# Decoder block on one core: front and attention in one program, first projections in another order, rotary turns later in the tails

## The reference, cut to what matters

```python
q = (rms_norm(cq, q_norm_w[l]) @ w_uq[l]).reshape(b, s, N_HEADS, QK_NOPE_DIM + QK_ROPE_DIM)
q_nope, q_rope = q[..., :QK_NOPE_DIM], q[..., QK_NOPE_DIM:]
kv = (rms_norm(ckv, kv_norm_w[l]) @ w_ukv[l]).reshape(b, s, N_HEADS, QK_NOPE_DIM + V_DIM)
k_nope, v = kv[..., :QK_NOPE_DIM], kv[..., QK_NOPE_DIM:]
q_rope = apply_rope(q_rope, cos[:, :, None, :], sin[:, :, None, :])
k_rope = apply_rope(k_pe, cos, sin)
o = mla_attention(q_nope, q_rope, k_nope, k_rope, v)   # causal softmax((qn.kn + qr.kr) * scale) @ v
y_b = (o * jax.nn.silu(b_gate)) @ w_attn_out[l]
```

## Time and profile before

| | us |
|---|---|
| median of 3 runs | 2596.09 (2595.48 to 2596.93) |
| the profiled execution's own time | 2595.87 |
| its span, first to last instruction | 2594.0 |
| PE busy | 2535.4 (98%) |
| DVE busy | 1709.9 (66%) |
| ACT busy | 875.0 (34%) |
| POOL busy | 689.2 (27%) |

### The profile page before, as it was taken

The page is one execution under the profiler, slowest core; times in us unless marked ns, Lnnn a source line. Parts: engine busy times, 40 slices in busy tenths (PEclk is TensorE's granted clock), DMA queues, the critical chain, the costliest instruction groups (busy, mean ns, idle before and its releaser), DMA issues. The chain is left out here.

```text
span 2594.0 us, 30760 instructions
## 1 busy us (share of the span) xinstructions
PE 2535.4 (98%) x12058; PEld 2092.6 (81%) x12058; DVE 1709.9 (66%) x2025; ACT 875.0 (34%) x1735; POOL 689.2 (27%) x621
## 2 busy tenths in 40 slices
PE   5999999999999999999999999999999999999998
PEld 4788888888888888788878888888888788888887
DVE  5678787989889898657466676676677522223343
ACT  3552111111111111133455655655656521111221
POOL 2223111111111111133133333333344310323422
PEclk9999999999999999999999999999999999999999
DMA  8023321313213121179824214214213264757532
GB/s 310 25 94 122 91 57 58 91 49 90 57 58 90 49 83 57 62 242 305 297 100 143 82 68 139 82 68 138 82 69 103 84 229 138 224 203 234 188 138 81
DMA packets 193180, 316.48 MB, mean 122 GB/s; under 512 B 14249, under 2 KB 107501, under 8 KB 182412
## 3 DMA queue, kind: packets, MB, share of 16 engines
q1 hardware_dynamic: 183164, 289.08, 34.2%
q0 software_dynamic: 5120, 16.78, 2.0%
q10 hardware_dynamic: 4752, 8.65, 0.9%
HBM read 207.52 MB, written 106.95 MB: 121 GB/s over the span
## 5 line engine op out<-in xcount | busy, mean ns | idle before, releaser
L52 PE MATMUL ps_proj<-h_hi,w_hi 128*128 128x512 f32 x1664 | 655.5, 394 | 9.2 <-DVE h_lo L937 6.8
L54 PE MATMUL ps_proj<-h_hi,w_lo 128*128 128x512 f32 x1664 | 648.8, 390 | 0.0
L53 PE MATMUL ps_proj<-h_lo,w_hi 128*128 128x512 f32 x1664 | 648.7, 390 | 0.0
L1046 DVE SCALAR_TENSOR_TENSOR acc<-u,taps_t,acc 128x2048 f32<-128x2048 f32 x240 | 628.9, 2621 | 8.5
L829 POOL TENSOR_TENSOR w_lo<-raw,w_hi 128x1024 fp32r<-128x1024 f32 x52 | 175.0, 3365 | 808.2 <-ACT w_hi L558 808.2
L52 PEld LDWEIGHTS ps_proj<-h_hi,w_hi 128*128 128x128 f32 x1664 | 312.9, 188 | 77.1 <-issue 7.5
L54 PEld LDWEIGHTS ps_proj<-h_hi,w_lo 128*128 128x128 f32 x1664 | 313.0, 188 | 65.6
L53 PEld LDWEIGHTS ps_proj<-h_lo,w_hi 128*128 128x128 f32 x1664 | 313.2, 188 | 65.3 <-issue 1.9
L2033 POOL TENSOR_SCALAR prob<-prob,rinv 128x512 f32<-128x512 f32 (+2 forms) x320 | 199.8, 642 | 348.3 <-DVE rinv L1916 345.3
L1977 DVE TENSOR_TENSOR pt_lo<-ps_t,pt_hi 128x512 fp32r<-128x512 f32 (+1 forms) x320 | 192.7, 607 | 76.6 <-ACT pt_hi L1894 72.8
L1960 DVE TENSOR_REDUCE nmax<-ps_ring 128x1 f32<-128x512 f32 (+3 forms) x288 | 176.2, 622 | 95.0 <-PE ps_ring L1760 77.0
(11 more groups left out here) (272 smaller groups left out, 4044.4 us busy)
## 6 DMA issues: line engine op xcount, KB each, us to landing
qlat<-qlat_dram SPq DMA_DIRECT2D x32, 1024.0 KB, 7.6
raw<-in_w_in_dram SPq DMA_DIRECT2D x52, 512.0 KB, 6.4
under_h<-in_w_ada_dram SPq DMA_DIRECT2D x8, 1024.0 KB, 10.7
ga_dram<-lat SPq DMA_DIRECT2D x8, 1024.0 KB, 5.0
gb_dram<-lat SPq DMA_DIRECT2D x8, 1024.0 KB, 5.2
agate_dram<-lat SPq DMA_DIRECT2D x8, 1024.0 KB, 5.0
conv_dram<-acc SPq DMA_DIRECT2D x8, 1024.0 KB, 3.9
v_dram<-v_st SPq DMA_DIRECT2D x4, 2048.0 KB, 8.9
```

The lines of the kernel that those rows point to most:

```text
L52: pe.matmul(out, wh, xh, start=first, stop=False)
L53: pe.matmul(out, wh, xl, start=False, stop=False)
L54: return pe.matmul(out, wl, xh, start=False, stop=last)
L1046: dve.scalar_tensor_tensor(acc[:], u[:, n:n + S], tap(n), acc[:], ALU.mult, ALU.add).then_inc(conv_tap if n < TAPS - 1 else conv_done, 1)
```

## The change

Front and attention no longer have blocks of their own. Each phase function now only defines its five engine programs, and one block runs on every engine first the front's and then the attention's, with no barrier between. In its place TensorE waits, at the first use of each of its eight banks in attention, for the front's unit that held it (`k.front_bank_free`), and ahead of the first scores for the loads of the rotated key (`k.rotary_key_in`). SyncE still waits at the end of the front's program for the front's transfers, as before; the semaphores of attention are taken from the shared set. The output phase keeps its block.

The first projections come in another order (`FIRST`): those of chunk 3's queries stand before the last two key chunks. The rotary turns stand behind units named in `TURNED`: chunk 2's behind `("QN", 3)`, chunk 3's behind `("K", 2)`, so that behind `("K", 3)` there is none; the one-column Exp with its table load follows the turn of chunk 3. On SyncE `queries(3)` is issued ahead of `store_values(1)`.

In the tail of a second body the turn of chunk 2 and `VS 0` leave the tiles: four T follow `QN 2`, then `QN 3`, `VS 0`, and the whole turns of chunk 2 and chunk 3. TensorE's order stays the same.

The rest of the diff is indentation; without it and without the signatures that change alike it is:

```diff
+Programs = namedtuple("Programs", "sync tensor scalar vector gpsimd")
...
-    FIRST = [(kind, c) for c in range(NC_) for kind in ("QR", "QN", "K")]
+    FIRST = [("QR", 0), ("QN", 0), ("K", 0), ("QR", 1), ("QN", 1), ("K", 1), ("QR", 2), ("QN", 2), ("QR", 3), ("QN", 3),
+             ("K", 2), ("K", 3)]
+    TURNED = {("K", 0): 0, ("K", 1): 1, ("QN", 3): 2, ("K", 2): 3}
...
             store_second(1)
-            store_values(1)
             queries(3)
+            store_values(1)
             rotary_key(1, k.kr_lo2)
...
-                if kind == "K":
-                    if n == 0:
+                if (kind, n) in TURNED:
+                    if TURNED[kind, n] == 0:
                         stage_stored(act)
-                    turn_rows(n)
-            act.activation(k.rsum[:, 0, 0:1], k.eps[:], ACT.Exp)
+                    turn_rows(TURNED[kind, n])
+                    if TURNED[kind, n] == NC_ - 1:
+                        act.activation(k.rsum[:, 0, 0:1], k.eps[:], ACT.Exp)
...
+        def bank_free(pe, b):
+            held = [e for n, e in enumerate(UNITS) if V_BANKS[n % len(V_BANKS)] == b][-1]
+            if held[0] == "V":
+                pe.wait_ge(v_done[held[1] % 2], held[1] // 2 + 1)
+            else:
+                pe.wait_ge(f.proj_free, FIRST.index(held) + 1)
+
+        k.front_bank_free = bank_free
...
-                between = [[("K", 3)], [("QN", 2)], [], [("QN", 3)]]
+                between = [[("K", 3)], [("QN", 2)], []]
             for c, then in enumerate(between):
-                if c == NC_ - 1 and not queries:
-                    tiles(2)
-                    ev += then + [("RS", c), ("RB", c), ("RH", c), ("RL", c)]
+                if c == 2 and not queries:
+                    tiles(4)
+                    ev += [("QN", 3), ("VS", 0)]
+                    for late in (2, 3):
+                        ev += [("RS", late), ("RB", late), ("RH", late), ("RL", late)]
                     break
...
+                    if begun and n == 0:
+                        pe.wait_ge(k.rotary_key_in, 64)
+                    if begun and n < RING:
+                        k.front_bank_free(pe, n)
                     ring_wait(at, n)
...
+                if begun and n < 2:
+                    k.front_bank_free(pe, RING + n)
...
+                if begun and n == 0:
+                    k.front_bank_free(pe, RING + 2)
...
+        with nc.Block() as block:
+            @block.sync
+            def _(sp):
+                k.front.sync(sp)
+                k.attention.sync(sp)
...
+            @block.tensor
+            def _(pe):
+                k.front.tensor(pe)
+                k.attention.tensor(pe)
...
```

More of the change, by code:

```diff
@@ L8 @@
+from collections import namedtuple
 from contextlib import ExitStack
@@ new lines, in front_phase @@
+        k.front = Programs(sync, tensor, scalar, vector, gpsimd)
+        def bank_free(pe, b):
+            held = [e for n, e in enumerate(UNITS) if V_BANKS[n % len(V_BANKS)] == b][-1]
+            if held[0] == "V":
+                pe.wait_ge(v_done[held[1] % 2], held[1] // 2 + 1)
+            else:
+                pe.wait_ge(f.proj_free, FIRST.index(held) + 1)
+        k.front_bank_free = bank_free
+        k.front_sems, k.last_values_out, k.rotary_key_in = sems, v_out[V_AT[-1]], next_in
@@ new lines, in gpsimd, with run @@
+        def gpsimd(pool):
+            pool.sem_inc(w_hi_made, 1)
+            pool.sem_inc(w_lo_made, 1)
+            pool.sem_inc(t_done, T_CREDIT)
+            pool.sem_inc(pv_done, PV_CREDIT)
+            def run(ev, at):
+                for kind, n in ev:
+                    if kind == "W":
+                        pool.wait_ge(w_hi_made, at.per(1, 2))
+                        pool.tensor_tensor(wl[:], raw[:], wh[:].bitcast(F32), ALU.subtract).then_inc(w_lo_made, 1)
+                    elif kind == "RP":
+                        s = slice(n * TC, (n + 1) * TC)
+                        pool.wait_ge(rows_in, at.per(48, 48))
+                        pool.tensor_tensor(qb[:, s], qb[:, s], k.trig[:, s], ALU.mult).then_inc(rope_step, 1)
+                    elif kind == "OW":
+                        pool.wait_ge(next_w_hi, n + 1)
+                        pool.tensor_tensor(k.o_w_lo[n][:], k.o_raw[n][:], k.o_w_hi[n][:].bitcast(F32),
+                                           ALU.subtract).then_inc(next_w_lo, 1)
+                    elif kind == "VB":
+                        pool.wait_ge(v_hi_made, n + 1)
+                        pool.tensor_tensor(v_lo[:, n * QB:(n + 1) * QB, :], v_raw[n][:],
+                                           v_hi[:, n * QB:(n + 1) * QB, :].bitcast(F32), ALU.subtract).then_inc(v_lo_made, 1)
+                    elif kind == "VS":
+                        pool.wait_ge(v_hi_made, at.per(NC_, (NC_ if n < 2 else 0) + n + 1))
+                        v = slice(n * QB, (n + 1) * QB)
+                        pool.tensor_tensor(v_lo[:, v, :], v_raw[n % 2][:], v_hi[:, v, :].bitcast(F32),
+                                           ALU.subtract).then_inc(v_lo_made, 1)
+                    elif kind == "E":
+                        g, b = BLOCKS[n]
+                        pool.wait_ge(rinv_done, at.block(n + 1))
+                        pool.sem_inc(passed, 1)
+                        if ev is opening and n == len(BLOCKS) - 1:
+                            pool.wait_ge(values_stored, 1)
+                            nc.clear_and_free_semaphores(k.front_sems)
+                        for c in range(g + 1):
+                            width = TC if c < g else (b + 1) * P
+                            x = (p_at(g, b) + c * QB) * P
+                            pool.tensor_scalar(prob[:, x:x + width], prob[:, x:x + width], rinv[:, n:n + 1], 1.0,
+                                               ALU.mult, ALU.mult).then_inc(normed, 1)
+            for i in range(PAIRS - 1):
+                run(first_body if i else opening, At(i, 0))
+                run(second_body, At(i, 1))
+            run(second_body, At(PAIRS - 1, 0, N_SECOND))
+            run(last_body, At(PAIRS - 1, 1, N_SECOND))
@@ L2043, in output_phase @@
+        k.attention = Programs(sync, tensor, scalar, vector, gpsimd)
 def output_phase(k):
@@ L2385, in _ @@
                 finish(finished)
-PHASES = ("front", "attn", "output")
 ATTN_HELD = 2 * LT * S + S + 2 * 2 * LT * TC + 3 * LT * 3 * P
@@ L2392, with build @@
 V_ST = H * 4 * VD
-def build(nc, ins, out, phases=PHASES):
+def build(nc, ins, out):
     with ExitStack() as ctx:
@@ L2450, in build, with _ @@
             k.raw = [hctx.enter_context(nc.sbuf_tensor(f"raw{i}", [P, KT, P], F32)) for i in range(2)]
[L2451 to L2459 removed]
+            k.shared = ctx.enter_context(ExitStack())
+            k.sems = Begun(lambda n: k.shared.enter_context(nc.semaphore(n)))
+            front_phase(k)
+        attention_phase(k)
+        with nc.Block() as block:
[7 more added lines that the diff above has]
+                k.attention.tensor(pe)
+            @block.scalar
+            def _(act):
+                k.front.scalar(act)
+                k.attention.scalar(act)
+            @block.vector
+            def _(dve):
+                k.front.vector(dve)
+                k.attention.vector(dve)
+            @block.gpsimd
+            def _(pool):
+                k.front.gpsimd(pool)
+                k.attention.gpsimd(pool)
+        k.shared.close()
+        output_phase(k)
 _INS = ["x", "c", "positions", "w_ada", "b_ada", "norm_w", "w_in", "conv_w", "conv_b", "conv_ln_w", "conv_ln_b",
```

2538 lines of the change are left out of this document (1234 added, 1304 removed).

## The result

| | median us | lowest to highest | runs |
|---|---|---|---|
| kernel before | 2596.16 | 2594.33 to 2599.93 | 12 |
| changed kernel | 2604.36 | 2598.62 to 2607.58 | 12 |

What follows compares the result with a forecast made beforehand. TensorE, busy 98% of the 2594.0 us span, was taken as the bound. Boundary -3.4, tails +8.9 and clock +3.0 gave +8.5 us, to 2604.5; range 2596 to 2609.

Steps and rivals of the forecast that it cites:

- The boundary: Front to attention: removing the barrier gains 5.6 us, of which the wait for v_raw leaves 3.4.
- Rival (b): Boundary: v_raw is in time, 2.2 us more gained and one gap less; +5.5, 2601.5 us; chance 0.10.
- The front's new order: First projections: VectorE loses 0.8 us at the rope_rows copy, TensorE nothing; counted as nothing, range 0 to 1 us.
- The tails: Four second-body tails: late turns delay the next head's block 4; 2.22 us lost per tail, +8.9 in all.
- The clock: Five new TensorE gaps: half followed by 1.2 GHz, +3.0 us; bounds 0 and 6.0.
- (a): Tails: late turns are hidden and block 4 doesn't wait; -5.9 us, 2590; chance 0.13.
- (c): Tails: no collision of RB with POOL, 1.65 us per tail, few clock drops; +3.5, 2599.4 us; chance 0.12.
- (d): Every new TensorE gap brings a clock drop; +11.5 us, 2607.6; chance 0.10.

Runs made afterwards that it cites:

- experiment one: Changed kernel with the second bodies' tails as before (chunk 2's turn and VS 0 among the tiles): 2593.32 us, ratio 0.9985.
- experiment three: Changed kernel with the tails as before and the first two v_raw loads issued ahead of the front's last 2 MB store: 2589.51 us, ratio 0.9971.
- seven: Kernel before, with chunk 2's turn spread between the tail's last tiles and VS 0 behind chunk 3's turn: 2593.49 us, ratio 0.9988.
- eight: Changed kernel with chunk 2's turn spread between the last tiles, VS 0 behind chunk 3's turn, and early v_raw loads: 2585.11 us, ratio 0.9956.
- experiment five: Changed kernel, only GpSimd's v_lo of VS 0 in second bodies held until all four chunks are turned: 2600.63 us, ratio 1.0014.
- two: Kernel before with only the changed kernel's tails of the second bodies: 2607.64 us, ratio 1.0044.
- six: Changed kernel with the old front order, turn places, SyncE order and tails, leaving only the barrier's removal: 2594.81 us, ratio 0.9994.
- four: Changed kernel with VS 0 behind both late turns instead of ahead of them: 2595.74 us, ratio 0.9994.

## Why the prediction was right, and where it wasn't

The mechanism and the sum held: +8.2 measured beside +8.5. Term by term:

- **The boundary, -3.4.** Right, to a few tenths: 3.40 in the trace and 3.6 between the medians of experiment one. The gap was 2.08 (2.2 forecast) and ended as forecast, by the exponent behind the value conversion behind v_raw; experiment three took it away and got 2.26 us. Rival (b), v_raw in time, came only with that reordering of the queue.
- **The front's new order, nothing.** The copy to rope_rows waited 2.05 us, not 0.8. Counted from the last value matmul, VectorE came to it 0.7 us earlier than I had worked out, and the store landed 0.6 later. TensorE lost nothing that can be seen: from the matmul of 1101.43 to the last value matmul it is 197.12 us here and 196.61 before, and between 195.3 and 198.4 in the other runs.
- **The tails, +8.9.** The gap (2.38 forecast as about 2.4), its end by RL of chunk 3, RB's 1.22 (1.25 forecast) and its end 0.54 behind GpSimd (0.55) came out. The chain from RS 2 to the end of RL 3 took 5.36 us; forecast was 5.38. One tail without a slow stretch costs 2.05, not 2.22. The wait for GpSimd that I had put at 0.5 is there, but half of it stands elsewhere: in head 6 the second chunk of block 4 comes 0.23 late, and the first turned tile 0.24. More is saved ahead of the gap: 1.07, not 0.6. I had priced RB 2's place ahead of pt_lo, but not the slow RL of the old tail, whose 1.81 us I had read in the earlier trace rows: of the other 0.44, 0.30 lies in the two products with the values that stand behind it. Another 1.2 in all comes back later. The four tails thus cost 7.0 us without the clock (10.3 less the 3.3 of the next point). This term was too high by 1.9.
- **The clock, +3.0.** Too low by about as much. I took half of the five gaps; in the profiled execution four of the five brought 1.2 GHz, three in tails (3.32, 2.90 and 3.20 less 2.05 each, together 3.3, so 1.1 each as forecast) and one at the boundary at about 1.5: 4.8 us. What was off is how many of the gaps it follows. This is the slowest of the twelve executions; by the medians the tails cost 11.0, which leaves 4.0 for the clock in them, so it isn't this execution alone. That the slow clock hides part of itself was right: without it the first turned tile follows the scores by 0.31 us, with it by 0.07.
- **The rivals.** (a) needed RL 3 by 1499.7 on the old scale; it came as late as worked out, and experiments one, seven and eight show that without late turns the kernel is faster. (c) fell with the 1.22 and with experiment five, which made its case by hand: 2600.63, beside 2599.4. (d) comes near: nearly every gap brought a drop in the profiled execution, but the tails themselves were cheaper.

Small slips of the working didn't matter: ScalarE comes to the conversion at 1303.5 on the old scale (1309.11 - 5.6), not 1303.7, and 2596.09 + 8.5 is 2604.6.

So the forecast hit to 0.3 us, but two of its terms were off by just under 2 us each, in opposite directions. That part of the hit is luck; the boundary and the length of the gaps are not.

What stays open: which gaps bring a slow stretch, and how often in the executions without a profile. The changed kernel's twelve runs spread over 9.0 us, those of experiment eight over 2.1. No trace shows them, but the mean granted clock of each is on record. Nine of the twelve have 0.995 to 0.998, and the time rises as it falls: 2598.6 us at 0.998, 2600.5 to 2604.0 at 0.997, 2603.2 and 2606.6 at 0.996, 2606.5 to 2607.6 at 0.995. The other three, 2602.2 at 0.992 and 2604.7 and 2605.0 at 0.991, are in the same order among themselves; a second level some 0.005 lower is found among the executions of every kernel, in the kernel before without a difference of 1 us in time. A slow stretch of some 3 us lowers the mean by about 0.0006 (3 x 0.5 / 2600, an estimate), so a number of slow stretches that varies from run to run fits, and the profiled execution had many.

## What to carry to other kernels

Removing a barrier is worth what the next wait leaves of it: follow each engine past the barrier, and ask of what was just stored and is at once loaded again whether its load can be issued ahead of the last big store. A chain of operations that go to and fro between two engines has a latency that no engine's busy share shows; before it is moved late, add it up to the instruction that waits for it, and spread it between pieces of other work where it needn't be in one. With a small piece for GpSimd, look at what VectorE does in the same microsecond.

## What the runs showed of the hardware that was not expected

Whether a gap of TensorE brings 1.2 GHz is not told by its length alone. One profiled execution of each kernel gives:

| gap, us | kernel and place | followed by 1.2 GHz |
|---|---|---|
| 3.87 | before, two and seven: first scores | 3 of 3 |
| 2.79, 2.81 | changed kernel, five: the gap at 79.27 of the earlier trace rows | 2 of 2 |
| 2.63 | six: first scores | no |
| 2.38 | changed kernel, block 4 | 3 of 4 |
| 2.38 | two, block 4 | 3 of 4 |
| 2.38 | six: the gap at 79.27 | yes |
| 2.27 to 2.34 | the other seven: the gap at 79.27 | 0 of 7 |
| 2.21 | all ten: the gap at 1101.43 of the earlier trace rows | 10 of 10 |
| 2.08 to 2.10 | changed kernel and five: sixth block | 2 of 2 |
| 2.09 to 2.10 | one and four: sixth block | 0 of 2 |
| 1.85 | five, block 4 | 2 of 4 |
| 1.32 | four, block 4 | 0 of 4 |

The gap of 2.21 at one place was followed by it every time, and slightly longer ones at another place never. The sixth block's gap is the same wait with the same work around it in all four kernels of its two rows. In the changed kernel the window behind it stands at 0.50 (above); in experiment one, at the same place, at 1.00:

```profile
1314.00:1315.00 1.00, 1.00 (x7) 0.79 (x5) 0.69 (x1) 0.94 (x5) 0.06 (x1) 1.00 0.72 242
```

And 256 KB of v_raw took 7.2 us to land in the changed kernel, behind a store of 2 MB that was issued 1.5 us earlier, and 2.7 in experiment three, ahead of it.
